# Decoder step: the norm between out-projection and FFN from per-token sums, normed in pairs of tiles, with the first FFN block run k-major

## The chip, the cores and the metric

The kernel runs on one core of one Trainium2 chip. The metric is the device time of one execution in microseconds (us), lower is better. The engines are named as in the profile: PE is TensorE, ACT is ScalarE, DVE is VectorE, POOL is GpSimd, SP is the queue that loads the weights.

## What is computed

One layer of a decoder for 320 tokens (256 of a prompt, 64 of eight short sequences, each sequence with its own modulation vector), width 2048, in f32. Between the mixer and the FFN the reference does this:

```
def rms_norm(x, g):
    return x * rsqrt(mean(x * x, axis=-1) + EPS) * g

m = jnp.concatenate([a, pooled], axis=-1) @ w_out          # out-projection
x = x + gate1 * rms_norm(m, g_post)                        # residual
h = rms_norm(x, g_pre_ffn) * (1.0 + scale2) + shift2
f = jnp.square(jax.nn.relu(h @ w1)) @ w2                   # FFN, 2048 -> 8192 -> 2048
y = x + gate2 * rms_norm(f, g_post_ffn)
```

The six modulation vectors come from `silu(c) @ w_ada + b_ada`. Since rms_norm(m, g) is a row factor rstd1 times m times g, the sum of squares of the new x is sum(x*x) + 2 rstd1 sum(x*mg) + rstd1^2 sum(mg*mg), with mg = gate1 * g_post * m.

## The kernel before

Channels lie on the 128 partitions and tokens on the free axis: a matrix of activations is 16 tiles of 128 channels x 320 tokens, and a norm over channels is a sum over tiles and over partitions. Every product is done in three passes of a split f32: ACT rounds a half chunk of weights (128 x 1024) from `raw` to `w_hi` (L356), DVE subtracts to get `w_lo` (L684), and PE multiplies w_hi by the high and the low part of the activations and w_lo by the high part (L1294). One chunk of 128 output channels is 2 halves x 8 k-tiles x 3 = 48 matmuls with 320 columns. There are four raw slots, four w_hi and four w_lo buffers, so weights are prepared one chunk ahead; SP loads a slot again once `slot_used` says that both w_lo halves (or the PE, for a modulation chunk) have read it, strictly in the order of the stream.

The modulation weights are streamed between the products: `ada_chunk` (L1272) multiplies one raw chunk as it is, four make a block of 512 channels, and `ada_turn` transposes it (L1281).

Order of the work: input projection, attention, pooling; then `x` is loaded again by a DMA on POOL's queue (L1200), since its memory was used by the pooling; then four groups of the out-projection (`super4`, each with four product chunks and one modulation block); then the norm; then the FFN, four groups of 16 up chunks and 16 down chunks. Every engine runs its own written-out program and waits on semaphores, so what stands in a queue before a waiting instruction is not overtaken.

The stretch that is changed, before the change:

- Out-projection, each tile: ACT copies the bank to `back` (L547) and squares it to `out_sq` (L549), DVE adds that to `sq_sum` (L976); at each group DVE and POOL multiply `back` by the gate (L980, L1208).
- After the last tile: PE sums `sq_sum` over the partitions with a matrix of ones, result wide on 320 columns (L1245), ACT takes the root (L344), DVE the reciprocal over 320 columns (L662). `update_x` then multiplies `back` by it (L294) and adds it to `x` (L295), eleven tiles on DVE and five on POOL. ACT squares x (L577), PE sums the squares (L1255, L1262), DVE and ACT multiply by the gain (L1004, L572), a second root and reciprocal follow, then `times_rstd` (L666), shift and rounding to `h_hi` on ACT (L586), `h_lo` on DVE (L1018) in four groups of four tiles.
- FFN: the first block of four chunks is `plain4`, each chunk over all 16 k-tiles. Its first half needs the first two groups of h, its second half the others. ACT evacuates a chunk with a relu (L594), DVE squares it and splits it (L1029, L1031, L1032). Banks 0 and 1 alternate.
- POOL then zeroes `back` (L1237), in which the FFN's output is summed later.

## Time and profile before

| | |
|---|---|
| median of 3 runs | 1533.31 us (1529.58 to 1538.15) |
| span of the profiled execution | 1529.8 us |
| mean granted TensorE clock | 0.982 of full speed |
| PE busy | 1452.8 us, 95% |
| DVE busy | 780.9 us, 51% |
| ACT busy | 497.5 us, 33% |
| POOL busy | 129.6 us, 8% |

The profiled execution's span lies at the low end of the three runs, 3.5 us under their median. All times of rows are counted from the start of the span. "Idle before" in square brackets is how long the engine stood before an instruction and what released it. A granted clock of 1.00 is 2.4 GHz, 0.50 is 1.2 GHz.

### The profile page before, as it was taken

What the parts mean: (1) busy time and instruction counts of PE and PEld (TensorE: products, weight loads), DVE (VectorE), ACT (ScalarE), POOL (GpSimd) and SP (SyncE); (2) the same over time, 40 slices, a digit from 0 to 9 for tenths busy, and PEclk for the clock granted to TensorE, in tenths of its full rate; (3) what the DMA queues carried; (4) which work ended last, traced back from release to release, by engine and by line L of the source; (5) the groups of instructions that cost most, each with busy time, mean ns of one, the idle gap of its engine ahead of it and who ended that gap; (6) DMA issues with size and microseconds to landing.
All of it is one profiled execution on the core that took longest, in us unless ns stands there. A gap on an engine that the chain in (4) does not pass through costs nothing.

```text
span 1529.8 us, 27305 instructions
## 1 busy us (share of the span) xinstructions
PE 1452.8 (95%) x10284; PEld 1317.9 (86%) x10284; DVE 780.9 (51%) x1163; ACT 497.5 (33%) x685; POOL 129.6 (8%) x176
## 2 busy tenths in 40 slices
PE   5999999999899966999999999999999999999994
PEld 1777777777788836999998999999999999999994
DVE  2555557846633467544333554433554434455556
ACT  2222234442432333333332333322333232333331
POOL 2000000167200043000000000000000000000003
PEclk9999999999999977999999999999999999999997
DMA  9999989889587752445445544345544445544421
GB/s 367 335 326 322 322 296 332 286 306 369 188 301 262 242 205 95 153 141 162 145 157 193 193 137 165 138 163 190 190 141 163 138 157 184 192 151 140 162 82 69
DMA packets 87711, 316.02 MB, mean 207 GB/s; under 512 B 12160, under 2 KB 12288, under 8 KB 87024
## 3 DMA queue, kind: packets, MB, share of 16 engines
q1 hardware_dynamic: 79056, 287.87, 54.2%
q0 software_dynamic: 5216, 22.51, 3.9%
q10 hardware_dynamic: 3392, 5.01, 0.9%
q8 instruction: 30, 0.49, 0.1%
q14 instruction: 17, 0.14, 0.0%
HBM read 309.56 MB, written 5.80 MB: 206 GB/s over the span
## 4 chain that ended last, share of the span: by engine, by line
PE 81%; DVE 7%; DMA 6%; issue 2%; ACT 2%; POOL 2%; POOLq 1%; SPq 0%; DVEq 0%; ACTq 0%
PE bank L1294 68%; PE bank L1356 6%; PE bank L1272 4%; DMA raw<-in_stream 4%; DMA k_pages<-in_kc 1%; DVE back L294 1%; DVE w_lo L684 1%; DVE x L295 1%; DMA pools_out<-u_s 1%; ACT w_hi L356 1%; POOL win L1153 1%; PE bank L1281 1%; DVE h_lo L1018 0%; POOLq L1134 0%; DVE rstd L662 0%
## 5 line engine op out<-in xcount | busy, mean ns | idle before, releaser
L356 ACT ACTIVATE w_hi<-raw 128x1024 fp32r<-128x1024 f32 x352 | 362.6, 1056 | 355.3 <-PE bank L1294 231.6
L684 DVE TENSOR_TENSOR w_lo<-raw,w_hi 128x1024 fp32r<-128x1024 f32 x352 | 418.4, 1222 | 112.7 <-ACT w_hi L356 111.0
L1294 PE MATMUL bank<-h_hi,w_hi 128*128 128x320 f32 x1280 | 402.2, 314 | 13.3 <-DVE h_lo L1018 10.0
L1294 PE MATMUL bank<-m_hi,w_hi 128*128 128x320 f32 x1280 | 397.5, 311 | 0.7 <-DVE w_lo L684 0.7
L1294 PE MATMUL bank<-h_lo,w_hi 128*128 128x320 f32 x1280 | 397.6, 311 | 0.0
L1294 PE MATMUL bank<-h_hi,w_lo 128*128 128x320 f32 x1280 | 397.5, 311 | 0.0
L1294 PE MATMUL bank<-m_lo,w_hi 128*128 128x320 f32 x1280 | 395.8, 309 | 0.0
L1294 PE MATMUL bank<-m_hi,w_lo 128*128 128x320 f32 x1280 | 395.8, 309 | 0.0
L1294 PEld LDWEIGHTS bank<-h_hi,w_hi 128*128 128x128 f32 x1280 | 242.1, 189 | 42.0 <-issue 38.5
L1294 PEld LDWEIGHTS bank<-m_hi,w_hi 128*128 128x128 f32 x1280 | 240.3, 188 | 14.5 <-issue 12.9
L1294 PEld LDWEIGHTS bank<-h_lo,w_hi 128*128 128x128 f32 x1280 | 242.2, 189 | 0.0
L1294 PEld LDWEIGHTS bank<-h_hi,w_lo 128*128 128x128 f32 x1280 | 242.1, 189 | 0.0
L1294 PEld LDWEIGHTS bank<-m_lo,w_hi 128*128 128x128 f32 x1280 | 240.4, 188 | 0.0
L1294 PEld LDWEIGHTS bank<-m_hi,w_lo 128*128 128x128 f32 x1280 | 240.3, 188 | 0.0
L1039 DVE TENSOR_TENSOR back<-bank,back 128x320 f32 (+1 forms) x64 | 31.4, 491 | 238.4 <-PE bank L1294 238.4
L1029 DVE TENSOR_TENSOR relu<-relu 128x320 f32<-128x320 f32 x64 | 31.5, 492 | 223.3 <-ACT relu L594 223.3
L594 ACT ACTIVATE relu<-bank 128x320 f32<-128x320 f32 x64 | 28.0, 438 | 317.7 <-PE bank L1294 317.7
L1272 PE MATMUL bank<-raw,silu_c 128*9 128x512 f32 x768 | 109.7, 605 | 6.5 <-DMA raw<-in_stream 6.4
L294 POOL TENSOR_TENSOR back<-back,rstd 128x960 f32<-128x960 f32 (+1 forms) x4 | 12.4, 3107 | 920.7 <-DVE rstd L662 920.7
L1356 PE MATMUL bank<-h_hi,w_hi 128*128 x256 | 83.4, 326 | 4.5 <-DVE w_lo L684 3.7
L1356 PE MATMUL bank<-h_hi,w_lo 128*128 x256 | 79.8, 312 | 0.0
L1356 PE MATMUL bank<-h_lo,w_hi 128*128 x256 | 79.7, 311 | 0.0
(187 smaller groups left out, 909.7 us busy)
## 6 DMA issues: line engine op xcount, KB each, us to landing
raw<-in_stream SPq DMA_DIRECT2D x544, 512.0 KB, 5.0
k_pages<-in_kc POOLq DMA_DIRECT2D x16, 512.0 KB, 9.1
v_pages<-in_vc POOLq DMA_DIRECT2D x16, 512.0 KB, 6.4
x<-in_x_cm ACTq DMA_DIRECT2D x1, 2560.0 KB, 12.2
x<-in_x_cm POOLq DMA_DIRECT2D x1, 2560.0 KB, 11.3
v_out<-v_cm POOLq DMA_DIRECT2D x1, 1280.0 KB, 9.8
k_out<-back POOLq DMA_DIRECT2D x1, 1280.0 KB, 10.0
y_out<-x SPq DMA_DIRECT2D x2, 640.0 KB, 3.0
```

The source lines that it names most:

```text
L294: mine.then(eng.tensor_tensor(part, part, rstd[:, :].unsqueeze(1).to_broadcast([P, end - first, T]), ALU.mult))
L295: eng.tensor_tensor(x[:, first:end, :], x[:, first:end, :], part, ALU.add).then_inc(done, 1)
L356: act.activation(w_hi[2 * (j % 2) + h][:, :], raw[slot][:, h * 1024:(h + 1) * 1024], ACT.Copy).then_inc(hi_ready, 1)
L594: freed(act.activation(relu[j % 2][:, :], bank[j % 2][:, 0:T], ACT.Relu), j)
L684: dve.tensor_tensor(w_lo[q][:, :], raw[slot][:, h * 1024:(h + 1) * 1024], w_hi[q][:, :], ALU.subtract).then_inc(slot_used[slot], 1)
L1029: mine.then(dve.tensor_tensor(relu2[j % 2][:, :], relu[j % 2][:, :], relu[j % 2][:, :], ALU.mult))
L1039: dve.tensor_tensor(tile, bank[j % 2][:, 0:T], tile, ALU.add).then_inc(bank_free[j % 2], 1)
L1153: mine.mark(pool.tensor_tensor(dst[:, start:UP], src_p[:, start:UP], src_p[:, start - back_by:UP - back_by], ALU.add))
L1272: last = pe.matmul(ADA[32 * kk:32 * kk + NSEQ, :], silu_c[:, 4 * a + kk, :], raw[slot][:, kk * 512:(kk + 1) * 512], start=(a == 0), stop=( ...
L1281: last = pe.transpose(MODT[:, t * P:(t + 1) * P], ada_rows[:, t * P:(t + 1) * P], ident)
L1294: last = pe.matmul(bank[j % 2][:, 0:T], w[q][:, k * P:(k + 1) * P], v[:, 8 * h + k, :], start=(h == 0 and k == 0 and n == 0), stop=(h == 1 ...
L1356: last = pe.matmul(QUARTER_BANKS[2 * h + i][:, 0:T], w[q][:, (4 * i + k) * P:(4 * i + k + 1) * P], v[:, ds(4 * g + k, 1), :].rearrange("p ...
```

## The change

- Sums: in the out-projection each tile now also yields sums of x*x, x*mg and mg*mg. ACT squares x (`scale_x`) and the gated tile, DVE multiplies and adds. ACT and POOL also store `x_scaled` and `m_scaled`, x and mg times (1+scale2)*g_pre_ffn. All this needs x, so ACT, POOL and DVE read the reloaded x from the first tile on.
- After the last tile PE sums the four totals to 3 columns of 128 tokens each, ACT and DVE take the two roots on 3 elements a partition, and PE spreads each result to 320 columns (`widen`).
- h is then (m_scaled*rstd1 + x_scaled)*rstd2 + shift, in eight pairs of tiles, all of it on DVE but the shift and rounding of the prompt part.
- First FFN block: the four chunks are cut by k, each holding 4 k-tiles for all four output tiles; four banks are summed at once, and each pair of h tiles is used when it is ready. `w_lo` of its chunks 2 and 3 is made by POOL. Three of its modulation chunks come ahead of the sums on PE, the fourth after chunk 1.
- The residual itself (back*rstd1, x+back, then the zeroing of back) is done by POOL once the last pair is ready, in eight operations of 4 tiles (1280 elements a partition).

```diff
+        def scale_x(n):
+            act.wait_ge(x_sq_summed, n)
+            act.activation(x_sq[:, :], x[:, n, :], ACT.Square).then_inc(x_squared, 1)
+            act.activation(x_scaled[:, n, 0:NP_], x[:, n, 0:NP_], ACT.Copy, scale=scale2[:, n, 0:1]).then_inc(x_scaled_p, 1)
...
+            act.wait_ge(sq_summed, n + 1)
+            act.activation(out_sq[j % 2][:, :], bank[j % 2][:, 0:T], ACT.Square).then_inc(out_squared, 1)
+            act.wait_ge(sample_gated, n + 1)
+            freed(act.activation(back[:, n, 0:NP_], bank[j % 2][:, 0:NP_], ACT.Copy, scale=gate[:, n, 0:1]), j)
+            act.wait_ge(bank_free[j % 2], 2 * c4 + (BANK_LEAD + j // 2 + 2))
+            act.wait_ge(gated_summed, n)
+            act.activation(gated_sq[:, :], back[:, n, :], ACT.Square).then_inc(gated_squared, 1)
+            act.activation(m_scaled[:, n, 0:NP_], back[:, n, 0:NP_], ACT.Copy, scale=scale2[:, n, 0:1]).then_inc(m_scaled_p, 1)
...
-        first_of_mlp = (FFN_C4, ffn_use(0) + 1, PLAIN[0], 0)
-        with act.Fori(0, OUT_GROUPS - 1) as t:
-            block4(OUT_C4 + t, out_use(t), SUPER, (OUT_C4 + 1 + t, out_use(t + 1), SUPER[0], 0), evac_out, t, SHIFT2 + t)
-        t = OUT_GROUPS - 1
...
+        act.wait_ge(x_again, 16)
+        act.wait_ge(gate_done, 6)
+        for t in range(OUT_GROUPS):
+            for j in range(4):
+                for h in range(2):
+                    hi_half(*out_next(t, j), h)
+                if j == 3:
+                    ada_copy(SHIFT2 + t, out_use(t), 6)
+                scale_x(4 * t + j)
+                wait_chunk(act, OUT_C4 + t, j)
+                evac_out(OUT_C4 + t, j, t)
...
+        act.wait_ge(tokens_summed, 1)
+        act.activation(root_t, SQ_SUMS, ACT.Sqrt, bias=eps, scale=1.0 / KT).then_inc(rooted, 1)
+        act.wait_ge(total_done, 1)
+        act.activation(root_t, total_t, ACT.Sqrt, bias=eps, scale=1.0 / KT).then_inc(rooted, 1)
...
+            act.wait_ge(pair_done, g + 1)
+            for i in range(2):
+                k = 2 * g + i
+                act.activation(h_hi[:, k, 0:NP_], u[:, i, 0:NP_], ACT.Identity, bias=shift[:, k, 0:1])
+            act.wait_ge(pair_shifted, g + 1)
+            act.activation(h_hi[:, 2 * g:2 * g + 2, NP_:T], u[:, :, NP_:T], ACT.Copy).then_inc(ffn_hi, 1)
...
+        hi_half(*first_chunk(1), 0)
+        pair_hi(0)
+        hi_half(*first_chunk(1), 1)
+        pair_hi(1)
+        pair_hi(2)
         for h in range(2):
-            hi_half(*first_of_mlp, h)
...
+            hi_half(*first_chunk(2), h)
+        for g in range(3, 6):
+            pair_hi(g)
+        ada_copy(GATE2, ffn_use(0), FIRST_ADA[3])
+        for h in range(2):
+            hi_half(*first_chunk(3), h)
+        for g in range(6, PAIRS):
+            pair_hi(g)
...
-                block4(c4, use + 1, PLAIN, (c4 + 1, use + 2, 0, 0), lambda c, j, t: evac_ff1(g, c, j, t), 0)
+                for h in range(2):
+                    hi_half(c4 + 1, use + 2, 0, 0, h)
+                for j in range(4):
+                    act.wait_ge(half_free, 8 * c4 + 4 + 7 + j // 2)
+                    evac_ff1(g, c4, j, 0, FIRST_BANKS)
...
+            n = 4 * t + j
+            dve.wait_ge(x_squared, n + 1)
+            add_to(x_sq_sum, x_sq[:, :], n, x_sq_summed)
+            dve.wait_ge(out_squared, n + 1)
+            dve.tensor_tensor(seq_view(back[:, n:n + 1, NP_:T]), seq_view(bank[j % 2][:, NP_:T].unsqueeze(1)),
+                              bcast_seq(gate[:, n:n + 1, :]), ALU.mult).then_inc(sample_gated, 1)
+            add_to(sq_sum, out_sq[j % 2][:, :], n, sq_summed, 2)
             wait_evac(c4, j)
...
+            dve.tensor_tensor(x_gated[:, :], x[:, n, :], back[:, n, :], ALU.mult).then_inc(crossed, 1)
+            dve.wait_ge(crossed, n + 1)
+            add_to(cross_sum, x_gated[:, :], n, cross_summed)
+            dve.wait_ge(gated_squared, n + 1)
+            add_to(gated_sum, gated_sq[:, :], n, gated_summed)
...
-        update_x(dve, mine, "dve", x_dve)
...
+        for t in range(OUT_GROUPS):
+            for j in range(4):
+                for h in range(2):
+                    lo_half(*out_next(t, j), h)
+                evac_out(OUT_C4 + t, j, t)
+            if t + 1 < OUT_GROUPS:
+                mod_add(SHIFT2 + t)
...
+        mine.then(dve.tensor_tensor(total_t, SUMS[:, 9:12], rstd1_t, ALU.mult))
+        mine.then(dve.scalar_tensor_tensor(total_t, SUMS[:, 6:9], 2.0, total_t, ALU.mult, ALU.add))
+        mine.then(dve.tensor_tensor(total_t, total_t, rstd1_t, ALU.mult))
+        mine.then(dve.tensor_tensor(total_t, SUMS[:, 3:6], total_t, ALU.add))
+        dve.tensor_scalar(total_t, total_t, 0.0, None, ALU.max).then_inc(total_done, 1)
...
+            dve.tensor_tensor(mixed[:, :, :], m_scaled[:, tiles, :], two_of(RSTD1), ALU.mult).then_inc(pair_mixed, 1)
...
+            dve.tensor_tensor(mixed[:, :, :], x_scaled[:, tiles, :], mixed[:, :, :], ALU.add).then_inc(pair_mixed, 1)
...
+            dve.tensor_tensor(pair[g % 2][:, :, :], mixed[:, :, :], two_of(RSTD2), ALU.mult).then_inc(pair_done, 1)
+            dve.wait_ge(pair_done, g + 1)
+            part = seq_view(pair[g % 2][:, :, NP_:T])
+            dve.tensor_tensor(part, part, bcast_seq(shift[:, tiles, :]), ALU.add).then_inc(pair_shifted, 1)
...
+            dve.wait_ge(ffn_hi, g + 1)
+            for i in range(2):
+                k = 2 * g + i
+                dve.scalar_tensor_tensor(h_lo[:, k, 0:NP_], pair[g % 2][:, i, 0:NP_], shift[:, k, 0:1], h_hi[:, k, 0:NP_],
+                                         ALU.add, ALU.subtract)
+            dve.tensor_tensor(h_lo[:, 2 * g:2 * g + 2, NP_:T], pair[g % 2][:, :, NP_:T], h_hi[:, 2 * g:2 * g + 2, NP_:T],
+                              ALU.subtract).then_inc(h_ready, 1)
...
+        for g in range(PAIRS):
+            if g == 3:
+                mod_add(SHIFT2 + 3)
+                dve.wait_ge(mod_done, SHIFT2 + 3 + 2)
+            if g in (1, 2):
+                lo_half(*first_chunk(1), g - 1)
+            elif g + 1 < PAIRS:
+                pair_gated(g + 1)
+            pair_lo(g)
+            if g in (1, 2):
+                pair_gated(g + 1)
+            if g + 1 < PAIRS:
+                pair_scaled(g + 1)
+        dve.tensor_copy(rstd[:, :], RSTD1).then_inc(rstd1_copied, 1)
...
-                block4(c4, use + 1, PLAIN, (c4 + 1, use + 2, 0, 0), lambda c, j, t: evac_ff1(g, c, j, t), 0)
+                for h in range(2):
+                    lo_half(c4 + 1, use + 2, 0, 0, h)
+                for j in range(4):
+                    evac_ff1(g, c4, j, 0)
+                mod_add(GATE2)
...
+        pool.wait_ge(gate_done, 6)
+        pool.wait_ge(x_again, 16)
...
+            pool.tensor_tensor(seq_view(x_scaled[:, tiles, NP_:T]), seq_view(x[:, tiles, NP_:T]), bcast_seq(scale2[:, tiles, :]),
+                               ALU.mult).then_inc(x_scaled_s, 1)
...
+        for c in (2, 3):
+            c4, use, off, j = first_chunk(c)
+            slot, _ = use_of(use, off)
+            for h in range(2):
+                pool.wait_ge(hi_ready, 8 * c4 + (2 * j + h + 1))
+                q = 2 * (j % 2) + h
+                pool.tensor_tensor(w_lo[q][:, :], raw[slot][:, h * 1024:(h + 1) * 1024], w_hi[q][:, :],
+                                   ALU.subtract).then_inc(slot_used[slot], 1)
...
-        pool.wait_ge(sample_gated, 4)
-        pool.wait_ge(x_again, 16)
-        update_pieces(0, 4)
...
+        pool.wait_ge(rstd1_copied, 1)
+        pool.wait_ge(h_ready, 4 + PAIRS)
         for g in range(4):
             tiles = slice(4 * g, 4 * g + 4)
-            pool.tensor_tensor(seq_view(normed[:, tiles, NP_:T]), seq_view(x[:, tiles, NP_:T]), bcast_seq(gate[:, tiles, :]),
-                               ALU.mult).then_inc(sample_times_gain, 1)
-        for pair in range(2):
-            for g in (2 * pair, 2 * pair + 1):
-                pool.wait_ge(normed_s, 4 + g + 1)
-                part = seq_view(normed[:, 4 * g:4 * g + 4, NP_:T])
-                pool.tensor_tensor(part, part, bcast_seq(mod[:, SHIFT2 + g, :, :]), ALU.add).then_inc(sample_mod, 1)
-            pool.wait_ge(sample_mod, 4 + 2 * pair + 2)
-            for g in (2 * pair, 2 * pair + 1):
-                tiles = slice(4 * g, 4 * g + 4)
-                pool.wait_ge(sample_hi, g + 1)
-                pool.tensor_tensor(h_lo[:, tiles, NP_:T], normed[:, tiles, NP_:T], h_hi[:, tiles, NP_:T],
-                                   ALU.subtract).then_inc(sample_lo, 1)
+            pool.tensor_tensor(back[:, tiles, :], back[:, tiles, :], rstd[:, :].unsqueeze(1).to_broadcast([P, 4, T]),
+                               ALU.mult).then_inc(residual_scaled, 1)
+            pool.wait_ge(residual_scaled, g + 1)
+            pool.tensor_tensor(x[:, tiles, :], x[:, tiles, :], back[:, tiles, :], ALU.add).then_inc(residual_added, 1)
+        pool.wait_ge(residual_added, 4)
         pool.memset(back[:, :, :], 0.0).then_inc(back_zeroed, 1)
-        update_pieces(1, 4 + KT)
...
-        pe.wait_ge(sq_summed, 2 + KT)
-        mean_of_sum()
-        for a in range(4):
-            ada_chunk(GATE2, ffn_use(0), a, a)
-        sum_parts(1)
-        ada_turn(GATE2)
-        mean_of_parts(1)
+        for a in range(3):
+            ada_chunk(GATE2, ffn_use(0), FIRST_ADA[a], a)
+        for n, (total, sem, need) in enumerate(((sq_sum, sq_summed, 2 + KT), (x_sq_sum, x_sq_summed, KT),
+                                                (cross_sum, cross_summed, KT), (gated_sum, gated_summed, KT))):
+            pe.wait_ge(sem, need)
+            sums = SUMS[:, 3 * n:3 * n + 3] if n else SQ_SUMS
+            for i in range(3):
+                last = pe.matmul(sums[:, i:i + 1], total[:, TOKENS[i]:TOKENS[i] + P], ones[:, 0:1],
+                                 start=True, stop=True)
+            last.then_inc(tokens_summed, 1)
...
+            pe.wait_ge(rstd_s, turn)
+            for i in range(3):
+                picked = ident[:, 64:P] if i == 2 else ident
+                last = pe.matmul(out[:, i * P:min(T, i * P + P)], row[:, i:i + 1].to_broadcast([P, P]), picked,
+                                 start=True, stop=True)
+            last.then_inc(done, 1)
+        widen(RSTD1, rstd1_t, 2, rstd1_wide)
+        widen(RSTD2, rstd2_t, 3, rstd2_wide)
...
+        for c in range(4):
+            c4, use, off, j = first_chunk(c)
+            slot, u = use_of(use, off)
+            for h in range(2):
+                pe.wait_ge(slot_used[slot], 2 * u + (3 + h))
+            for k in range(4):
+                if k % 2 == 0:
+                    pe.wait_ge(h_ready, 4 + 2 * c + k // 2 + 1)
+                for i in range(4):
+                    q, at_k = 2 * (j % 2) + i // 2, (4 * (i % 2) + k) * P
+                    for n, (w, v) in enumerate(((w_hi, h_hi), (w_hi, h_lo), (w_lo, h_hi))):
+                        last = pe.matmul(FIRST_BANKS[i][:, 0:T], w[q][:, at_k:at_k + P], v[:, 4 * c + k, :],
+                                         start=(c == 0 and k == 0 and n == 0), stop=(c == 3 and k == 3 and n == 2))
+                    if k == 3 and i % 2:
+                        last.then_inc(half_free, 1)
+            if c == 1:
+                ada_chunk(GATE2, ffn_use(0), FIRST_ADA[3], 3)
+            if c == 2:
+                ada_turn(GATE2)
```

## Rows read from the trace of the kernel before

**Rows 1.** Chain that ended last: page, by engine; and in time (start us, us)
```profile
PE 81%; DVE 7%; DMA 6%; issue 2%; ACT 2%; POOL 2%; POOLq 1%; SPq 0%; DVEq 0%; ACTq 0%
...
591.34 224.48 PE bank L1294 x1512
```

**Rows 2.** Timeline between the products: start us, us, engine, instruction, idle before
```profile
547.16 0.60 PE L1281 MATMUL bank<-tab,ada_rows 128*128 128x128 f32 x4
550.04 3.62 PE L1272 MATMUL bank<-raw,silu_c 128*9 128x512 f32 x32
...
582.50 0.60 PE L1294 MATMUL bank<-h_hi,w_hi 128*128 128x320 f32 x1 [10.04 <-DVE h_lo L1018]
...
591.34 0.64 PE L1294 MATMUL bank<-h_hi,w_hi 128*128 128x320 f32 x1 [3.24 <-DVE w_lo L684]
...
597.62 0.44 ACT L594 ACTIVATE relu<-bank 128x320 f32<-128x320 f32 x1 [5.69 <-PE bank L1294]
```

**Rows 3.** Timeline of DVE alone, the residual update
```profile
553.28 1.49 DVE L294 TENSOR_TENSOR back<-back,rstd 128x1280 f32<-128x1280 f32 x1
554.80 3.39 DVE L295 TENSOR_TENSOR x<-x,back 128x1280 f32<-128x1280 f32 x1
558.12 3.51 DVE L294 TENSOR_TENSOR back<-back,rstd 128x1280 f32<-128x1280 f32 x1
561.66 2.71 DVE L295 TENSOR_TENSOR x<-x,back 128x1280 f32<-128x1280 f32 x1
```

**Rows 4.** Timeline of POOL alone, the same stretch
```profile
553.41 3.43 POOL L294 TENSOR_TENSOR back<-back,rstd 128x960 f32<-128x960 f32 x1 [4.51 <-DVE rstd L662]
556.92 3.35 POOL L295 TENSOR_TENSOR x<-x,back 128x960 f32<-128x960 f32 x1
560.24 2.78 POOL L294 TENSOR_TENSOR back<-back,rstd 128x640 f32<-128x640 f32 x1
563.10 2.66 POOL L295 TENSOR_TENSOR x<-x,back 128x640 f32<-128x640 f32 x1
```

**Rows 5.** Start of the out-projection: timelines of ACT, POOL, PE, and x's DMA
```profile
414.34 2.00 ACT L356 ACTIVATE w_hi<-raw 128x1024 fp32r<-128x1024 f32 x2
...
414.46 0.60 POOL L1200 DMA_DIRECT2D x<-in_x_cm  x1 [15.13 <-issue]
...
DMA to landing us min/median/max: 11.3/11.3/11.3
...
422.02 1.05 PE L1272 MATMUL bank<-raw,silu_c 128*9 128x512 f32 x8
...
431.98 0.41 PE L1294 MATMUL bank<-m_hi,w_hi 128*128 128x320 f32 x1 [0.71 <-DVE w_lo L684]
```

**Rows 6.** Windows: stretch, us, PE busy (x), granted clock, DMA share, GB/s
```profile
40.00:44.00 4.00, 1.10 (x8) 0.98 1.03 410
44.00:48.00 4.00, 4.00 (x19) 0.59 1.03 408
```

**Rows 7.** DVE: groups by shape, 415 to 620 us (busy, mean ns, idle); last row timeline
```profile
L684 DVE TENSOR_TENSOR w_lo<-raw,w_hi 128x1024 fp32r<-128x1024 f32 x40 | 47.4, 1222 | 14.4 <-ACT w_hi L356 13.7 <-issue 0.5 <-DVE sq_sum L971 0.2
L1018 DVE SCALAR_TENSOR_TENSOR h_lo<-normed,mod,h_hi 128x256 fp32r<-128x256 f32 x16 | 9.4, 649 | 0.9 <-ACT h_hi L586 0.9
L666 DVE TENSOR_TENSOR normed<-normed,rstd 128x1280 f32<-128x1280 f32 x4 | 5.8, 1482 | 0.0
L1029 DVE TENSOR_TENSOR relu<-relu 128x320 f32<-128x320 f32 x4 | 2.0, 492 | 12.2 <-ACT relu L594 12.2
...
591.20 2.14 DVE L1018 SCALAR_TENSOR_TENSOR h_lo<-normed,mod,h_hi 128x256 fp32r<-128x256 f32 x4
```

**Rows 8.** Timeline near the start: small operations on DVE and ACT
```profile
8.65 0.17 ACT L330 ACTIVATE small<-bank 128x2 f32<-128x2 f32 x1 [2.50 <-PE bank L1313]
...
19.04 0.16 DVE L652 TENSOR_TENSOR small<-small 128x1 f32<-128x1 f32 x1 [11.13 <-DMA ada_bias<-in_bias]
19.24 0.15 DVE L653 TENSOR_SCALAR small<-small 128x1 f32<-128x1 f32 x1
```

209 lines of the change are left out of this document (106 added, 103 removed).

## The prediction

> **What bounds the kernel now.** I read the page first: PE holds 81% of the chain that ended last, and from 591.34 us on it is one unbroken run of 1512 matmuls in 224.48 us, 148.5 ns each, so a chunk of 48 takes 7.13 us [rows 1]. An idle engine elsewhere is worth nothing; what counts is where PE stands still. The timeline gives the one long stop that the change is about [rows 2]: the last product of the out-projection ends at 547.2 us (the transposes follow at 547.16), the first FFN matmul starts at 582.50, 35.3 us later, and after half a chunk PE stands again until 591.34, waiting for a w_lo that is queued behind the norm on DVE. The half chunk from 591.34 to the relu at 597.62 took 6.3 us instead of 24 x 0.1485 = 3.6: 2.7 us are the price of a start at half clock. The first FFN chunk ends at 597.6, so the fifth ends at 597.6 + 4 x 7.13 = 626.1 us. I compare both kernels there, at the point where PE may begin the sixth chunk at full rate; behind it nothing differs.
>
> In the stop DVE and POOL work on the residual, and their rows interlock [rows 3, 4]. POOL's product of 960 elements begins at 553.41, while DVE is in an operation until 554.77; it ends at 556.84, which is 2.07 us after DVE's end. DVE's next one starts at 554.80 and ends at 558.19, 1.35 us after POOL's end. So it goes on: POOL 558.19 to 560.27, DVE to 561.63, POOL to 563.02, DVE to 564.37. One works while the other stands, in turns, although each row looks long. Read so, POOL needs 2.07 us for 960 elements and 1.39 for 640, that is 2.16 ns an element.
>
> The Trainium skill (SBUF — State Buffer, "Who interferes with whom") calls this an exclusive lock held for a whole instruction, taken by GpSimd operations that read SBUF and by Vector ones with two SBUF inputs; a Vector operation with at most one SBUF input goes free. The rows show its first half. By its second half DVE's two products per pair that read rstd from PSUM could run beside POOL, which no row here shows.
>
> **Part 1, x is needed from the first tile.** ACT's new wait for the reloaded x stands ahead of the rounding of the second out-projection chunk; queued behind it are all of ACT's roundings and evacuations, and behind those DVE's subtraction and PE. That rounding now runs at 414.34, but x is issued at 414.46 and lands 11.3 us later, at 425.8 [rows 5]. Rounding 1.1 (half of the 2.00 of the same row) and subtraction 1.2 [rows 7], with one turn of POOL's new products between (256 elements, 0.6), give PE its first half at 428.7. It is free at 422.02 + 1.05 = 423.1. It stands 5.6 us, and where PE was idle for most of a stretch of 4 us the next one was granted 0.59 [rows 6], so I add the 2.7 of a slow start: 428.7 + 7.13 + 2.7, + 1.05 for the modulation chunk, = 439.6 us against 431.98 now [rows 5]. Cost 7.6 us; 4.9 if the clock stays up. The rest of the new work per tile hides: ACT has six operations of at most 0.44 [rows 2], DVE six of at most 0.49 [rows 7], with 2.1 and 2.4 for the weights 4.7 and 5.3 us, beside a PE cycle of 7.13 + 1.05 = 8.2. If that cover were gone it would cost the excess over 8.2.
>
> **Part 2, the way to the first FFN matmul.** Counted from the end of the last product: transposes 0.6, three modulation chunks at 3.62/4 each = 2.7 [rows 2], now 3.3 and ahead of the sums. Four sums of three one-column products each: no row shows one; 128-wide weights cost 0.15 in the transposes (0.60 for four), f32 products may be split into two passes, so a sum is between 0.45 and 0.9; I take 0.6: 5.7. Five operations on 3 elements at 0.2 (start to start 19.04 to 19.24), then root 0.17 and reciprocal 0.2 [rows 8]: 7.1. Spreading rstd2 runs beside two DVE operations on 640 elements, 0.82 each (between 0.49 for 320 and 1.48 for 1280 [rows 7]): 8.8. Product 0.8; ACT rounds two tiles 0.9 and the samples 0.3: 10.9; three h_lo operations 1.4 (four in 2.14, so 0.54 each [rows 7]): 12.3 us. Against 35.3 that is 23 us gained. Bounds 11 and 15.
>
> **Part 3, eight pairs.** DVE has per pair 3 x 0.82 + 0.3 + 1.4 = 4.2, and 0.3 of waiting for ACT: 4.5. PE needs 3.6 per pair, so DVE is now the pace. Seven further pairs 31.5, two w_lo 2.4, one modulation add 0.5: the last pair is ready 46.7 us after the last product. POOL's four w_lo of 1024 elements last 2.2 each [rows 4], 8.9 in all, and hold DVE at most that long. The nearest row with less: L1018 takes 649 ns in the mean and 0.54 alone, so 16 of them lost 1.7 us beside eight POOL operations of 256 elements, 4.4 us in all, 0.4 of their time. Between 3.5 and 8.9 I take the middle, 6: 52.7 us. In absolute time 547.2 + 7.6 + 52.7 = 607.5, PE's last 24 matmuls end at 611.1. Today the block of four chunks ends at 597.6 + 3 x 7.13 = 619.0 us. Up to here the change is 8 us ahead.
>
> By the second half of that rule of the Trainium skill two of the three long operations of a pair are never held, which would put the four w_lo at the low end, 3.5, and the end of the block at 608.6.
>
> **Part 4, the residual comes out of the stop, and into the FFN.** POOL starts its eight operations of 1280 elements with the last pair: 8 x 1280 x 2.16 ns = 22.1 us, one behind the other. DVE meanwhile has nothing but operations with two SBUF inputs or a copy: two w_lo for the fifth chunk, then for each of four tiles square, copy and subtract, then a modulation add, and only then the w_lo of the sixth chunk. With turns as in the residual now [rows 3, 4] each of the first eight waits for a POOL operation of 2.8 us. DVE's own work is 0.5 + 2 x 1.2 + 4 x 1.3 + 0.5 + 1.2 = 9.8, 9.2 with the slightly shorter rows behind a turn. So the sixth chunk starts 9.2 + 22.1 = 31.3 us after 607.5, at 638.8. PE has idled twice by then: before the fifth chunk, whose bank comes free with the third relu, which needs the first tile's split on DVE (about 15 us after the last pair), and again before the sixth. This second idle costs another slow start of 2.7: 641.5 against 626.1. The zeroing of `back` stands behind this and is needed 11 chunks later; nothing waits.
>
> **Sum.** +7.6 - 23.0 for parts 1 and 2, then -8 becomes +15.4 by part 4. Nothing after it differs, and PE, being the bound, can't catch up. The profiled execution (span 1529.8) would give 1545; against the median of the runs, 3.5 us above its span: 1533.3 + 15.4 = 1548.7, **1549 us**. With the good ends (clock stays up twice, -5.4; tail 11; POOL holding less in part 3) it is 1541, with the bad ones 1558.
>
> **Rivals.**
> A, the other side: DVE and POOL don't hold each other here. The price is decided at one place, DVE's queue behind the last pair. Then the last pair is ready at 601.5, PE ends the block at 605.1, waits 1.5 for the third relu, and the sixth chunk starts at 613.7, 12.4 us earlier than now: 1521 us. For it: only that the new operations are shorter on DVE's side (0.3 to 1.2 us) than those seen taking turns [rows 3]. Against it: four turns in a row without exception, with the very operation that is moved. It decides from the point where POOL's holds cost under 12 of their 28 us. 14%.
> B: the turns are there, but cost about half, because DVE has pauses of its own (waits for relu and for its previous step) in which POOL runs for free. 15.4 - 11 = +4: 1538 us. For it: three waits per tile. Against it: POOL always has a next operation queued, so a pause only lets it in sooner, and each turn is 2.8 us. 18%.
> C: the new tail is not short: 12 small PE sums split in passes and at half clock, since PE has little to do there, and the spread of rstd at half clock too: 3 to 5 us more, 1553. 14%.
> D: the change does what it says but the wait for x isn't felt, because PE is held by the stream of raw chunks anyway (0.71 us of idle at 431.98 [rows 5]): then +8, 1541. The row speaks against it, 0.71 is all the slack there is. It is within the range. 4%.
>
> **Chances.** Forecast 50%, A 14%, B 18%, C 14%, D 4%. The measurement of this kernel tells about 0.5% (7.7 us) from no change, so faster is under 1525.6 and slower over 1541.0. Faster: A, 0.15. Same: B and half of D, 0.19. Slower: the rest, 0.66. The range leaves A out and takes in B and C: 1528 to 1558.
>
> **What would show it.** In the changed kernel's trace: (1) the second out-projection chunk starts near 428.7 and the third near 439; (2) the first FFN matmul comes 11 to 15 us after the last out-projection product; (3) pairs of h_lo every 4.5 us, some at 6 to 7 beside POOL's w_lo; (4) behind the last pair, rows of DVE of 3 us for operations that take 0.5, each ending shortly after a POOL row of the residual, and an idle PE of about 10 us before the fifth chunk and 6 before the sixth. If the DVE rows there have their plain length, part 4 and with it the sign are wrong. If pairs come at under 4 us, part 3 is.

## The result and the profile after

The changed kernel takes 1548.35 us in the median (1544.96 to 1553.82, four runs) against 1532.17 us before (1529.58 to 1538.15, four runs). The ratio is 1.0105, 95% interval 1.0084 to 1.0125, so the change costs 13 to 19 us. The forecast of 1549 us was right. Its profiled execution has a span of 1546.3 us.

The page of the changed kernel, busy time by engine and the chain of waits. PE has as many matmuls as before, 10284: 36 rows of small ones in the norm have taken the place of 36 others. Of the 16.5 us of additional span 12.5 are idle PE (89.5 us against 77.0), and 4.0 are longer busy time (1456.8 against 1452.8), at a mean granted clock of 0.979 instead of 0.982. In the chain PE falls from 81% [rows 1] to 79%, and DVE rises from 7% to 8%.

```profile
span 1546.3 us, 27183 instructions
PE 1456.8 (94%) x10284; PEld 1326.4 (86%) x10284; DVE 825.3 (53%) x1259; ACT 517.0 (33%) x742; POOL 145.5 (9%) x176
...
PE 79%; DVE 8%; DMA 5%; issue 3%; POOL 2%; ACT 2%; POOLq 1%; SPq 0%; DVEq 0%; ACTq 0%
...
L1144 DVE TENSOR_TENSOR relu<-relu 128x320 f32<-128x320 f32 x64 | 39.6, 618 | 210.2 <-ACT relu L643 210.2
```

The last row is one of the operations behind the norm. Before, it took 492 ns [rows 7]; now the mean over the whole kernel is 618. A mean over 64 hides that three of them took 3.2 us each (3 x 2.7 / 64 = 127 ns).

**The start of the out-projection**, timelines of ACT, POOL and PE of the changed kernel (start, length, engine, line; in brackets the idle time before and what ended it). They answer to [rows 5].

```profile
428.55 2.00 ACT L384 ACTIVATE w_hi<-raw 128x1024 fp32r<-128x1024 f32 x2 [11.12 <-DMA x<-in_x_cm]
...
417.45 0.60 POOL L1319 DMA_DIRECT2D x<-in_x_cm  x1 [17.17 <-PE bank L1650]
...
425.01 1.05 PE L1394 MATMUL bank<-raw,silu_c 128*9 128x512 f32 x8
431.23 0.61 PE L1416 MATMUL bank<-m_hi,w_hi 128*128 128x320 f32 x1 [5.17 <-issue]
...
440.83 1.04 PE L1394 MATMUL bank<-raw,silu_c 128*9 128x512 f32 x8
```

ACT stood 11.1 us until x landed, and PE got its second chunk at 431.23. That chunk took 9.6 us (431.23 to 440.83) instead of 7.13. The windows of the same kernel show why: granted clock in the third column from the right.

```profile
432.00:436.00 4.00, 4.00 (x17) 4.00 (x16) 2.95 (x7) 2.27 (x5) 1.34 (x1) 0.50 0.91 317
436.00:440.00 4.00, 4.00 (x27) 4.00 (x26) 2.76 (x3) 1.73 (x4) 0.00 (x0) 0.93 0.35 139
```

After its stop PE worked at 0.50 (1.2 GHz) until about 436, then at full rate.

**From the last product to the first FFN matmul**, timeline of PE, changed kernel. It answers to [rows 2].

```profile
557.00 0.60 PE L1403 MATMUL bank<-tab,ada_rows 128*128 128x128 f32 x4
557.53 2.76 PE L1394 MATMUL bank<-raw,silu_c 128*9 128x512 f32 x24
560.22 0.83 PE L1670 MATMUL bank<-ones,sq_sum 128*128 128x1 f32 x6
...
563.00 1.52 PE L1679 MATMUL bank<-tab,small 128*128 128x128 f32 x6
564.80 1.54 PE L1679 MATMUL bank<-tab,small 128*128 128x128 f32 x6 [0.28 <-DVE small L1067]
569.79 0.60 PE L1700 MATMUL bank<-h_hi,w_hi 128*128 128x320 f32 x1 [3.45 <-DVE h_lo L1120]
```

The last product ends at 557.16; the first FFN matmul starts 12.6 us later instead of 35.2 (the 35.3 of the prediction counts from the start of the transposes). Each sum of three columns is six matmuls, and the four follow each other every 0.67 to 0.75 us.

**The pairs**, DVE and then POOL of the changed kernel:

```profile
578.51 0.82 DVE L1095 TENSOR_TENSOR mixed<-m_scaled,bank 128x640 f32<-128x640 f32 x1
579.36 2.65 DVE L1101 TENSOR_TENSOR mixed<-x_scaled,mixed 128x640 f32<-128x640 f32 x1
582.04 0.82 DVE L1107 TENSOR_TENSOR pair<-mixed,bank 128x640 f32<-128x640 f32 x1
582.89 1.48 DVE L1110 TENSOR_TENSOR pair<-pair,mod 128x128 f32<-128x128 f32 x1
...
586.63 0.82 DVE L1101 TENSOR_TENSOR mixed<-x_scaled,mixed 128x640 f32<-128x640 f32 x1
...
590.54 0.82 DVE L1101 TENSOR_TENSOR mixed<-x_scaled,mixed 128x640 f32<-128x640 f32 x1
```

```profile
578.91 5.32 POOL L1341 TENSOR_TENSOR w_lo<-raw,w_hi 128x1024 fp32r<-128x1024 f32 x2 [20.04 <-ACT w_hi L384]
```

A pair takes 3.91 us where nothing interferes (586.63 to 590.54). Beside POOL's w_lo the sum of two SBUF tiles waits (2.65 instead of 0.82), and so does the small addition (1.48 instead of 0.29), while the product at 582.04, which reads one of its inputs from PSUM, keeps its 0.82. The other two w_lo (from 594.87) give the same picture. The Trainium skill (SBUF — State Buffer, "Who interferes with whom") says so: a Vector instruction with at most one SBUF input doesn't contend, unless it runs in a two-port mode, in which it uses the port pair that it shares with GpSimd as well; copies and casts can enter such a mode. The rows before the change could not show that half of the rule; these do.

**Behind the last pair**, DVE and then POOL of the changed kernel:

```profile
604.50 0.28 DVE L1120 TENSOR_TENSOR h_lo<-pair,h_hi 128x128 fp32r<-128x128 f32 x1
604.70 0.48 DVE L1138 COPY rstd<-bank 128x320 f32<-128x320 f32 x1
605.10 5.11 DVE L737 TENSOR_TENSOR w_lo<-raw,w_hi 128x1024 fp32r<-128x1024 f32 x2
610.13 3.16 DVE L1144 TENSOR_TENSOR relu<-relu 128x320 f32<-128x320 f32 x1
613.33 2.88 DVE L1146 CAST m_hi<-relu 128x320 fp32r<-128x320 f32 x1
616.25 3.08 DVE L1147 TENSOR_TENSOR m_lo<-relu,m_hi 128x320 fp32r<-128x320 f32 x1
...
628.50 3.20 DVE L1144 TENSOR_TENSOR relu<-relu 128x320 f32<-128x320 f32 x1
631.73 4.22 DVE L1146 CAST m_hi<-relu 128x320 fp32r<-128x320 f32 x1
635.98 0.49 DVE L1147 TENSOR_TENSOR m_lo<-relu,m_hi 128x320 fp32r<-128x320 f32 x1
```

```profile
605.26 3.86 POOL L1354 TENSOR_TENSOR back<-back,rstd 128x1280 f32<-128x1280 f32 x1 [5.28 <-DVE rstd L1138]
609.20 3.74 POOL L1357 TENSOR_TENSOR x<-x,back 128x1280 f32<-128x1280 f32 x1
612.90 3.12 POOL L1354 TENSOR_TENSOR back<-back,rstd 128x1280 f32<-128x1280 f32 x1
616.11 2.88 POOL L1357 TENSOR_TENSOR x<-x,back 128x1280 f32<-128x1280 f32 x1
...
628.31 3.04 POOL L1357 TENSOR_TENSOR x<-x,back 128x1280 f32<-128x1280 f32 x1
631.40 4.37 POOL L1359 MEMSET back<- 128x5120 f32 x1
```

Read the two together: POOL's row ends at 616.02, DVE's at 616.21; POOL's at 618.99, DVE's at 619.33. Eight turns, each a whole POOL operation long, for DVE operations whose plain length is 0.33 to 0.49. The ninth long row, the CAST at 631.73, stands beside the MEMSET and ends with it. PE meanwhile, changed kernel:

```profile
620.01 0.63 PE L1416 MATMUL bank<-h_hi,w_hi 128*128 128x320 f32 x1 [11.39 <-ACT relu L643]
...
639.60 0.60 PE L1416 MATMUL bank<-h_hi,w_hi 128*128 128x320 f32 x1 [10.38 <-DVE w_lo L737]
```

Two stops, 11.4 and 10.4 us, which the kernel before doesn't have.

### The profile page after: what moved, and what is told of

The parts are those of the page before. It is cut to its first block, busy times and chain, and to the rows that moved or that the text cites. A ratio compares the mean times of both kernels' runs of the same rounds, so it can differ in the third digit from the quotient of the medians.

```text
span 1546.3 us, 27183 instructions
## 1 busy us (share of the span) xinstructions
PE 1456.8 (94%) x10284; PEld 1326.4 (86%) x10284; DVE 825.3 (53%) x1259; ACT 517.0 (33%) x742; POOL 145.5 (9%) x176
## 4 chain that ended last, share of the span: by engine, by line
PE 79%; DVE 8%; DMA 5%; issue 3%; POOL 2%; ACT 2%; POOLq 1%; SPq 0%; DVEq 0%; ACTq 0%
PE bank L1416 67%; PE bank L1474 6%; PE bank L1394 5%; DMA raw<-in_stream 4%; DVE w_lo L737 1%; DMA k_pages<-in_kc 1%; DMA pools_out<-u_s 1%; DVE m_hi L1146 1%; DVE relu L1144 1%; PE bank L1403 1%; ACT w_hi L384 1%; DVE mixed L1101 1%; DVE back L322 0%; POOL win L1272 0%; DVE x L323 0%
## 5 line engine op out<-in xcount | busy, mean ns | idle before, releaser
L1416 PE MATMUL bank<-h_hi,w_hi 128*128 128x320 f32 x1216 | 382.2, 314 | 21.8 <-ACT relu L643 11.4
L1416 PE MATMUL bank<-h_hi,w_lo 128*128 128x320 f32 x1216 | 377.5, 310 | 0.0
L1416 PE MATMUL bank<-h_lo,w_hi 128*128 128x320 f32 x1216 | 377.4, 310 | 0.0
L1416 PEld LDWEIGHTS bank<-h_hi,w_hi 128*128 128x128 f32 x1216 | 229.9, 189 | 49.8 <-issue 49.8
L1416 PEld LDWEIGHTS bank<-h_lo,w_hi 128*128 128x128 f32 x1216 | 230.1, 189 | 0.0
L1416 PEld LDWEIGHTS bank<-h_hi,w_lo 128*128 128x128 f32 x1216 | 229.8, 189 | 0.0
L1144 DVE TENSOR_TENSOR relu<-relu 128x320 f32<-128x320 f32 x64 | 39.6, 618 | 210.2 <-ACT relu L643 210.2
L322 POOL TENSOR_TENSOR back<-back,rstd 128x960 f32<-128x960 f32 (+1 forms) x2 | 6.2, 3109 | 893.0 <-DVE rstd L715 893.0
## 6 DMA issues: line engine op xcount, KB each, us to landing
x<-in_x_cm POOLq DMA_DIRECT2D x1, 2560.0 KB, 11.1
```

Source lines behind the costliest of these rows:

```text
L322: mine.then(eng.tensor_tensor(part, part, rstd[:, :].unsqueeze(1).to_broadcast([P, end - first, T]), ALU.mult))
L1144: mine.then(dve.tensor_tensor(relu2[j % 2][:, :], relu[j % 2][:, :], relu[j % 2][:, :], ALU.mult))
L1416: last = pe.matmul(bank[j % 2][:, 0:T], w[q][:, k * P:(k + 1) * P], v[:, 8 * h + k, :], start=(h == 0 and k == 0 and n == 0), stop=(h == 1 ...
```

## The experiments

Each kernel was timed together with the kernel before on the same chip; the ratio is to that one. Unless it says otherwise an experiment starts from the changed kernel (ratio 1.0105), and 0.001 of the ratio is 1.53 us. Intervals of a ratio are 0.0017 to 0.0044 to each side, so differences of two ratios are uncertain by 4 to 9 us; the traces carry the finer steps.

**1. The residual left out.** The eight POOL operations are gone, so the residual is missing from y.

```
-        for g in range(4):
-            tiles = slice(4 * g, 4 * g + 4)
-            pool.tensor_tensor(back[:, tiles, :], back[:, tiles, :], rstd..., ALU.mult)
-            pool.wait_ge(residual_scaled, g + 1)
-            pool.tensor_tensor(x[:, tiles, :], x[:, tiles, :], back[:, tiles, :], ALU.add)
-        pool.wait_ge(residual_added, 4)
```

> The changed kernel with POOL's eight residual operations behind the last pair left out (so y lacks the mixer's residual); the zeroing of back stays. Theory (each POOL operation holds one DVE operation for its 2.8 us, and DVE's queue is what PE waits for): in the changed kernel the sixth FFN chunk starts 34.8 us after the last pair, without the eight it starts at about 3.6 + 1.5 + 7.1 = 12.2 us, and one slow start of PE (3 us) goes too: 1548 - 25 = 1523 us. Rival B (DVE's own pauses absorb half): 1536. Rival x (the loss is in the wait for x and in the k-major block): within 3 us of 1548.

Measured: 1524.49 us, ratio 0.9954 (0.9937 to 0.9971), 23 us less than the changed kernel. PE's only stop behind the last pair is 2.4 us. DVE's w_lo and relu have their plain lengths; only a CAST that meets the memset is held (1.03 instead of 0.33). POOL's operations, which no one waits for until much later, cost the whole loss and more. Not all of the 23 us is their own time, though: without them the memset also runs 27 us earlier (603.98 instead of 631.40), where it holds the CAST by 0.7 us instead of 3.9.

**2. Half of the residual.** The four products stay, the four additions to x are left out, so y lacks the residual here too.

```
-            pool.wait_ge(residual_scaled, g + 1)
-            pool.tensor_tensor(x[:, tiles, :], x[:, tiles, :], back[:, tiles, :], ALU.add)
```

> The changed kernel with the four additions x + back of the residual left out (y lacks the residual), the four multiplications stay: half the dose. Theory: four turns of 2.8 us less, so -11 to -12 us, 1536. Rival (only the first tile's split matters, which five turns already hold): nearly all of the loss stays, within 4 us of 1548. Rival (few POOL operations are absorbed by pauses): about as fast as without any, 1525.

Measured: 1534.17 us, ratio 1.0011 (0.9994 to 1.0028), 14 us less than with all eight. The first stop is still there (11.34 us), the second gone: with four turns only the fifth chunk is late. The memset, now at 617.10, holds the CAST at 617.82 (3.82 us).

**3. ACT rounds one more chunk before it waits for x.**

```
-        act.wait_ge(x_again, 16)
-        act.wait_ge(gate_done, 6)
         for t in range(OUT_GROUPS):
             for j in range(4):
                 for h in range(2):
                     hi_half(*out_next(t, j), h)
+                if t == 0 and j == 0:
+                    act.wait_ge(x_again, 16)
+                    act.wait_ge(gate_done, 6)
```

> The changed kernel, ACT rounds the second out-projection chunk before it waits for x and gate. Theory: the second chunk starts without a stop (now 5.2 us, and 2.4 of slow clock behind it), the third waits 1 to 3 us for ACT, which evacuates late: 4 to 6 us gained, 1543. Rival (the stream of raw chunks holds PE there anyway): at most 1 us.

Measured: 1538.67 us, ratio 1.0041 (1.0024 to 1.0058), 10 us less. In the trace the second chunk follows without a stop, and PE waits 0.81 us for the third, against 0.71 before the change [rows 5]:

```profile
431.51 1.05 PE L1395 MATMUL bank<-raw,silu_c 128*9 128x512 f32 x8
433.37 0.42 PE L1417 MATMUL bank<-m_hi,w_hi 128*128 128x320 f32 x1 [0.81 <-DVE w_lo L738]
```

From its first product to its last the projection takes 132.5 us, as before the change (132.4), against 139.2 in the changed kernel: 6.8 us of the 10. Of the rest, 1.7 us lie ahead of the projection (first product at 416.07 against 417.77).

**4. The same residual, one operation for each FFN chunk.** Each POOL operation waits for a relu of its own, from the fifth chunk on.

```
+            pool.wait_ge(hidden, 2 + 5 + 2 * g)
             pool.tensor_tensor(back[:, tiles, :], back[:, tiles, :], rstd..., ALU.mult)
             pool.wait_ge(residual_scaled, g + 1)
+            pool.wait_ge(hidden, 2 + 6 + 2 * g)
             pool.tensor_tensor(x[:, tiles, :], x[:, tiles, :], back[:, tiles, :], ALU.add)
```

> The changed kernel with the same eight residual operations, each held back until one more FFN chunk is split (the fifth chunk on), so that POOL takes one turn of 2.8 us per chunk of 7.1 us, in which DVE works 3.7. Theory (turns cost only where DVE has no slack): all of the stop after the last pair goes, and 3.7 + 2.8 = 6.5 fits in 7.1: 1524 us, as without the residual, 1527 if some turns delay PE. Rival (the turns cost their full time wherever they are put, 22 us): 1546.

Measured: 1521.64 us, ratio 0.9921 (0.9893 to 0.9950), 28 us less. The turns are all there. DVE, then POOL, of this kernel:

```profile
621.36 5.13 DVE L737 TENSOR_TENSOR w_lo<-raw,w_hi 128x1024 fp32r<-128x1024 f32 x2
626.85 0.49 DVE L1144 TENSOR_TENSOR relu<-relu 128x320 f32<-128x320 f32 x1 [0.36 <-ACT relu L643]
```

```profile
621.61 3.79 POOL L1355 TENSOR_TENSOR back<-back,rstd 128x1280 f32<-128x1280 f32 x1 [20.01 <-DVE m_lo L1147]
628.60 3.81 POOL L1359 TENSOR_TENSOR x<-x,back 128x1280 f32<-128x1280 f32 x1 [3.19 <-DVE m_lo L1147]
```

DVE's w_lo takes 5.13 instead of 2.35, yet DVE is done 0.36 us before the next relu. DVE's slack in a chunk is 3.2 us (its idle time before a relu where POOL is quiet), one hold is 2.8, and PE doesn't stop. The memset behind them holds a CAST for 2.45 us (at 676.81), and that too fits: DVE still waits 1.02 us for the next relu. The same instructions and the same holds, in another place, are as cheap as none at all (experiment 1).

**5. Experiments 3 and 4 together.**

> Both mendings at once: the residual operations spread over FFN chunks, one per chunk, and ACT's rounding of the second out-projection chunk ahead of its wait for x. Theory: the two costs lie in different stretches and add up, 26.7 and 6.8 us: 1548.4 - 33.5 = 1515. Rival (PE comes earlier and meets the raw stream, or both stand for one cause): 1520 or more.

Measured: 1515.57 us, ratio 0.9877 (0.9833 to 0.9920). The two causes add nearly: 28 and 10 us apart, 35 together, within their uncertainty. This kernel is 1.2% faster than the one before the change.

**6. Two of the three modulation chunks behind the sums**, on top of 5.

```
-        for a in range(3):
-            ada_chunk(GATE2, ffn_use(0), FIRST_ADA[a], a)
+        ada_chunk(GATE2, ffn_use(0), FIRST_ADA[0], 0)
...
         widen(RSTD2, rstd2_t, 3, rstd2_wide)
+        for a in (1, 2):
+            ada_chunk(GATE2, ffn_use(0), FIRST_ADA[a], a)
```

> As the kernel with both mendings, and two of the three modulation chunks that PE does ahead of the sums now come behind the spreading of rstd2. Theory: the sums start 1.8 us sooner and the last of them is bound by gated_sum (ready 3 us after the last product) instead of PE: first FFN matmul 10.7 instead of 12.6 us after the last product, 1513. Rival (the later modulation chunks delay the raw slots 2 and 3, and the first block waits for its weights): 1515 or more.

Measured: 1512.81 us, ratio 0.9871 (0.9833 to 0.9909). The first FFN matmul comes 10.9 us after the last product instead of 12.6. The gain of 1.7 us shows in the trace; the ratio alone could not tell it.

**7. The turns in the kernel before.** Here the old kernel gets eight operations of the same shape on POOL, ahead of its memset. They scale `back`, which the memset then clears, so nothing that is computed changes.

```
+        for g in range(8):
+            part = back[:, 4 * (g % 4):4 * (g % 4) + 4, :]
+            mine.then(pool.tensor_tensor(part, part, rstd..., ALU.mult))
         pool.memset(back[:, :, :], 0.0).then_inc(back_zeroed, 1)
```

> The kernel before, with eight POOL multiplications of 1280 elements (back by rstd, whose values are thrown away by the zeroing that follows) added between POOL's last h_lo and its zeroing of back. Nothing of the change is in it. Theory (turns between POOL and DVE while PE waits for DVE's queue): 22 us of turns less some 2 to 4 us of DVE's slack, and a slow start of PE: 1532 + 20 = 1552, at least 1545. Rival B (half): 1543. Rival (the loss needs the k-major block, whose four banks come due at once): at most 1536.

Measured: 1547.25 us, ratio 1.0105 (1.0073 to 1.0137): as large a loss as that of the whole change, from eight instructions whose result nobody uses. DVE, then POOL:

```profile
590.20 10.04 DVE L1018 SCALAR_TENSOR_TENSOR h_lo<-normed,mod,h_hi 128x256 fp32r<-128x256 f32 x4
```

```profile
590.84 26.16 POOL L1239 TENSOR_TENSOR back<-back,rstd 128x1280 f32<-128x1280 f32 x8
```

The first row is 2.14 us long in the kernel before [rows 7]. The long rows of DVE from there to 617.27 contain 21 us of holds, of which 16 reached the end; the time is 5 us below the 1552 that I expected. The two traces show where the rest went. The first w_lo of the third FFN chunk starts at 617.27 instead of 599.38, 17.9 us later: the 21.0 of holds, less the 2.02 that DVE waited for a relu in any case (at 598.09 in the kernel before), less 1.0 because this execution reached the projection earlier. Before, that w_lo was ready 4 us ahead of PE, which takes another 4 off, and the start at half clock gives 1.8 back: the third chunk ends 15.7 us later (627.42 against 611.70).

**8. POOL without any w_lo**, on top of 6: DVE makes w_lo of the first block's chunks 2 and 3 as well.

```
-                pool.tensor_tensor(w_lo[q][:, :], raw[slot][:, h * 1024:(h + 1) * 1024], w_hi[q][:, :], ...)
...
+            if g in (3, 6):
+                lo_half(*first_chunk(g // 3 + 1), 0)
             pair_lo(g)
+            if g in (3, 6):
+                lo_half(*first_chunk(g // 3 + 1), 1)
```

> As the kernel with all three mendings, and DVE instead of POOL makes w_lo of the first block's chunks 2 and 3. Theory: POOL's four operations held DVE 5.7 us in the changed kernel's trace, DVE's own four take 4 x 1.2 = 4.9 us in its queue, so it is the same within 1 us: 1512. If POOL's work was free (rival: turns don't matter here), it is 5 us slower, 1518.

Measured: 1511.54 us, ratio 0.9862 (0.9824 to 0.9900), the fastest of all, though its distance to 6 is within the uncertainty. In the trace the last pair comes 44.7 us after the last product instead of 45.8. Giving POOL work to relieve DVE had gained nothing: what POOL took off DVE's queue (four times 1.22 us) it gave back in holds (5.7 us).

**9. The residual in 16 operations of half the size.**

```
-        for g in range(4):
-            tiles = slice(4 * g, 4 * g + 4)
+        for g in range(8):
+            tiles = slice(2 * g, 2 * g + 2)
```

> The changed kernel with the same residual in sixteen POOL operations of 2 tiles (640 elements) instead of eight of 4 tiles, at the same place. Theory (what counts is POOL's total time ahead of the w_lo of the sixth chunk, and DVE has 15 held operations before it): turns of 1.4 instead of 2.8 us, the fifth chunk may start 7 us sooner, the sixth at the same time; 1548 +- 2. Rival (the length of one hold counts, short ones slip into DVE's pauses): 1538.

Measured: 1539.35 us, ratio 1.0038 (1.0021 to 1.0056). My expectation of no change was wrong by 9 us. The turns are half as long and twice as many, as expected, for instance in DVE of this kernel:

```profile
615.68 1.82 DVE L1144 TENSOR_TENSOR relu<-relu 128x320 f32<-128x320 f32 x1
...
632.50 5.08 DVE L737 TENSOR_TENSOR w_lo<-raw,w_hi 128x1024 fp32r<-128x1024 f32 x2
```

POOL and PE:

```profile
636.56 4.37 POOL L1359 MEMSET back<- 128x5120 f32 x1
```

```profile
635.24 0.61 PE L1416 MATMUL bank<-h_hi,w_hi 128*128 128x320 f32 x1 [8.82 <-DVE w_lo L737]
```

But the sixth chunk starts at 635.24, 28.6 us behind the last pair instead of 34.8. With twice as many turns DVE comes through its whole queue while POOL works, so that only 15 of the 16 turns stand ahead of the first of the sixth chunk's w_lo; their holds add up to 19.0 us in the rows instead of 21.2. And the memset begins after the start, so it can't delay it: 3.9 us. Together 6.1 of the 6.2 us that the trace shows; the medians lie 9 us apart, with an uncertainty of some 4. Experiments 11 and 12 test the second term.

**10. Two residual operations for each chunk.**

```
+            pool.wait_ge(hidden, 2 + 5 + g)
             pool.tensor_tensor(back[:, tiles, :], back[:, tiles, :], rstd..., ALU.mult)
```

> The changed kernel with the residual spread, but two POOL operations (5.5 us) per FFN chunk, over four chunks instead of eight. DVE then has 3.7 + 5.5 = 9.2 us of work and holds per chunk of 7.1. Theory (only what exceeds the chunk is paid): 4 x 2.1 = 8 us less the lead of 2 to 4 us that DVE has: 1526, against 1521.6 with one per chunk. Rival (an average over many chunks decides, DVE catches up): 1522.

Measured: 1534.02 us, ratio 0.9998 (0.9981 to 1.0015), 8 us worse than expected. DVE of this kernel:

```profile
633.84 5.13 DVE L737 TENSOR_TENSOR w_lo<-raw,w_hi 128x1024 fp32r<-128x1024 f32 x2
...
643.15 5.13 DVE L737 TENSOR_TENSOR w_lo<-raw,w_hi 128x1024 fp32r<-128x1024 f32 x2
```

With two holds DVE's cycle is 9.3 us (633.84 to 643.15), 2.2 over the 7.1 that PE needs. Over four chunks that uses up DVE's lead, as expected. What I had left out is the memset right behind it: a CAST at 660.96 takes 4.07 us instead of 0.33 when the lead is gone, PE stops for 5.5 us, and the next start is at half clock (1.4 us). Read from the rows these are 3.7 + 1.4 of the 8 us; no run here takes the memset away from this form, and the rest stays open.

**11. The memset later.** POOL zeroes `back` only after the eighth chunk's relu.

```
+        pool.wait_ge(hidden, 2 + 8)
         pool.memset(back[:, :, :], 0.0).then_inc(back_zeroed, 1)
```

> The changed kernel, in which POOL zeroes back only after the eighth FFN chunk's relu instead of right behind the residual. Theory: in the changed kernel the memset (631.40, 4.37 us) holds DVE's CAST at 631.73 (4.22 instead of about 0.33), which stands ahead of the sixth chunk's w_lo. Moved away, that CAST takes its plain 0.33, the sixth chunk starts 31 us behind the last pair instead of 34.8, and the time falls by 3.9 us: 1544.5 against 1548.4, a ratio of about 1.0080 instead of 1.0105. Rival: the CAST is held by something else, or the memset merely stands where another wait would end as late (PE's slow start): no change, 1548, and the CAST still long. At its new place the memset can meet one DVE operation of a later chunk; DVE has no lead there yet, so up to 1 us of the gain may be lost, 1545.5.

Measured: 1544.99 us, ratio 1.0074 (1.0055 to 1.0092), 4.7 us less than the changed kernel by the ratios. DVE, then POOL:

```profile
635.50 0.33 DVE L1146 CAST m_hi<-relu 128x320 fp32r<-128x320 f32 x1
```

```profile
665.55 4.37 POOL L1360 MEMSET back<- 128x5120 f32 x1 [30.44 <-DVE m_lo L1147]
```

The CAST behind the last turn now takes 0.33 instead of 4.22, and the sixth chunk starts 30.9 us behind the last pair (639.48 against 608.55) instead of 34.8: 3.9 us, as expected. (The span of this profiled execution is 1546.3 too; its projection began 3.9 us later than the changed kernel's, see below.)

**12. The same with the 16 small operations of experiment 9.**

> The changed kernel with the residual in 16 operations of 640 elements (as in e9) and with the memset behind the eighth FFN chunk's relu. In e9 the memset began (636.56) after the sixth chunk had started (635.24), so by my reading its 3.9 us are not in the path there, and moving it should change nothing: the time of e9, 1539.4, ratio about 1.004, sixth chunk 28.6 us behind the last pair. Rival: e9 gained for another reason (the shorter turns themselves), and the memset costs it 3.9 us as it does the undivided form: then 1535.5, ratio 1.0015.

Measured: 1539.46 us, ratio 1.0048 (1.0030 to 1.0065), against 1.0038 in experiment 9: no gain. The sixth chunk starts 28.6 us behind the last pair, exactly as there. So the memset costs 3.9 us where it stands in front of that start and nothing where it doesn't, which is the second part of the explanation of experiment 9.

## Why the prediction was right

**Part 1, the wait for x.** Predicted 7.6 us. The first product of the projection came 3.0 us later in this execution (417.77 against 414.79), so the marks move by that: second chunk 428.7 + 3.0 = 431.7, found 431.23; third 439.6 + 3.0 = 442.6, found 441.8. The projection from first to last product is longer by 6.9 us. The slow start was put at 2.7; the chunk took 9.6 instead of 7.13, 2.5. Experiment 3 gives the time back. Rival D is out.

**Part 2, the tail.** Predicted 12.3 us to the first FFN matmul, measured 12.6. The four sums took 2.8 instead of 2.4. The products that spread a root take 1.5 us, but the second one lies beside DVE's two operations, as assumed, and the h_lo behind it took 1.1 instead of 1.4. Rival C, 3 to 5 us more, is out, although part of what it assumed came true: each small product is two rows, and the spreading ran at a granted clock of 0.50. In the trace of experiment 4, where the clock was still 1.00, the first spreading took 0.86 instead of 1.52, and the first FFN matmul came 12.55 us after the last product; so the clock costs little here.

**Part 3, the pairs: sized wrongly.** The last pair was put at 52.7 us after the last product and came at 47.6. POOL's holds were 5.7 us, near the 6 that I took. The low end of 3.5 didn't come, though the products that read PSUM were never held: a hold lasts until POOL's operation ends, and so it fell on whichever operation with two SBUF inputs came next. The pair was mis-sized: 4.5 us, measured 3.9. I took h_lo at 1.4, from 0.54 an operation [rows 7], but the three take 1.0 from start to start. The 0.54 was misread as time without POOL: the first of those four operations (at 591.20 in the kernel before) took 0.95 us beside POOL's last h_lo, which ran until 591.87, and without a hold an operation of 256 elements takes 0.44. The small addition takes 0.2 instead of 0.3, and the wait for ACT 0.18 instead of 0.3. Over seven pairs this makes 4.1 of the 5.1 us. It made the change look worse than it is.

**Part 4, the residual in turns.** The mechanism is as written: eight holds. The eight long rows less their plain lengths (2.35, 0.49 and 0.33) add up to 21.2 us; I had 22.1. But the sixth chunk started 34.8 us after the last pair instead of 31.3. The step that failed is "the zeroing of `back` stands behind this and is needed 11 chunks later; nothing waits". Nobody waits for its result; DVE's CAST waits for the engine. Experiment 11 measures that term at 3.9 us, in the trace and, within its uncertainty, in the time (4.7). The kernel before contains the same memset (591.81 to 596.18 us), and it did no harm there. DVE, then POOL, of the kernel before:

```profile
593.71 2.35 DVE L684 TENSOR_TENSOR w_lo<-raw,w_hi 128x1024 fp32r<-128x1024 f32 x2
```

```profile
591.81 4.37 POOL L1237 MEMSET back<- 128x5120 f32 x1
```

Two w_lo, with two SBUF inputs each, kept their plain length beside it; no CAST met it. The Trainium skill (SBUF — State Buffer, "Who interferes with whom") draws the line where these rows do: two SBUF inputs contend only with a GpSimd operation that reads SBUF, whereas a copy or cast can enter a two-port mode and then contends with GpSimd whatever that does. I had used the rule for POOL's reads only, and the prediction tells it without this exception: by its words a CAST, with its one SBUF input, would go free, but the CAST at 613.33 was held by POOL's product and the one at 631.73 by the memset. (The sum of part 4 counts the casts as held all the same.)

The stops themselves were put at about 10 and 6 us; they were 11.4 and 10.4, because the pairs were earlier and the memset later than I had it.

**The sum.** To the sixth chunk at full rate: a start 3.0 later, 6.9 us more for the projection instead of 7.6, the last pair 5.1 early, the turns 3.5 late: 641.5 + 3.0 - 0.7 - 5.1 + 3.5 gives 642.2, and the trace 639.6 + 2.7 = 642.3 us, against 626.1 before. Two errors, -5.1 and +3.5, nearly cancel, and a later start of 3.0 that I hadn't forecast makes up the rest. Behind that point both kernels need the same: 904.0 us (1546.3 - 642.3) against 903.7. (Both marks use the prediction's rates. Its 7.13 us for a chunk has the slow start of 591.34 averaged in; the later chunks take 7.04, from the relu at 612.17 to that at 619.21. The slow start at 639.60 cost 2.4, not 2.7. With these the marks are 642.0 and 625.8, and the difference is the same.) That the total hit within 1 us is therefore partly luck; that it was slower, and by which mechanism, isn't. Two numbers around the sum need care. The 3.5 us added for the median aren't all due to a low run: in the executions of this case the device time is 1.6 to 1.7 us longer than the span (1547.99 against 1546.3 here), which is about half of it. And the upper end of the range, 1558, has no sum: a tail of 15 and holds of 8.9 give 1554.

**The rivals.** A (no turns) falls with experiments 1, 2 and 7: the eight operations, with the memset that they push back, cost 23 us, and eight like them 16 in the old kernel. B (half the cost) falls with the rows behind the last pair: 21.2 us of holds, not 11.

**Open.** The 3.0 us ahead of the projection. In twelve traces of the changed kernel and its variants the first product of the projection comes between 415.6 and 422.8 us, in the two of the old code (before and experiment 7) at 414.8 and 413.8. The whole difference is there before the attention ends (384.89 against 381.91 for the same matmul): 1.2 us are a longer wait for the DMA of `k_pages` (1.86 against 0.68), the rest small waits for DVE before it. The code up to there is nearly the same, the DMA engines are 0.85 to 0.92 busy from 50 to 350 us, and the wait for `k_pages` varies in the twelve traces from none (four of them) to 3.8 us. So it may be the variation between executions, but all twelve lie on one side. No experiment here separates it. If it belongs to the change, the change costs some 3 us more than parts 1 to 4 explain: in the profiled pair they explain 13 of the 16 us.

## What to carry to other kernels

Work that is moved to an idle engine is free only if it doesn't shut out the engine it runs beside: here the residual on POOL cost nothing in one place and, with the memset behind it, 23 us in another, with the same instructions, because DVE's queue there was the one that PE waited for. Price such work by whole operations of the other engine (one POOL operation for each short DVE operation that reads two SBUF inputs or is a cast), compare it with the slack of DVE in each chunk, and spread it so that one hold falls into each slack. And include operations that nobody waits for: a memset whose result was needed eleven chunks later held a cast for 3.9 us.
